# Twenty-two experts' weights copied to bfloat16 ahead of the expert stage, output weights prepared beside the projections, u2 stored by the sync queue

## What is computed

```
ada   = silu(c) @ w_ada + b_ada                  # 6 rows of 1024: shift, scale, gate, twice
u     = LN(x) * (1 + scale1) + shift1
q,k,v,g,p = split(u @ w_in)                      # 5 blocks of 512 columns
r     = retention(rotary(q), rotary(k), v)       # 4 heads of 128, chunks of 128 tokens
mix   = [silu(g) * groupnorm(r) | pool(p) @ w_pool] @ w_out
x     = LN(ALPHA * x + gate1 * mix, ln1_w, ln1_b)
u2    = LN(x) * (1 + scale2) + shift2
y     = top-1 group of 4, top-2 of its 8 gated-MLP experts (32 experts, hidden 256)
out   = LN(ALPHA * x + gate2 * y, ln2_w, ln2_b)
```

## Time and profile before

| | us |
|---|---|
| time, median of 3 runs | 1021.09 (1010.62, 1021.09, 1047.54) |
| profiled execution, its own time | 1010.89 |
| profiled execution, span of the slowest core (core 1) | 1009.1 |
| spans of the 8 cores | 981.3 to 1009.1 |
| busy: PE, DVE, ACT, POOL | 654.3, 530.5, 332.4, 351.6 |
| DMA queues, share of 16 engines over the span: q0 (POOL's), q1 (SP's) | 57.7%, 14.8% |

### The profile page before, as it was taken

The page is one execution under the profiler, slowest core; times in us unless marked ns, Lnnn a source line. Parts: engine busy times, 40 slices in busy tenths (PEclk is TensorE's granted clock), DMA queues, the critical chain, the costliest instruction groups (busy, mean ns, idle before and its releaser), DMA issues.

```text
span 1009.1 us, 11200 instructions; the slowest of 8 cores (981.3 to 1009.1 us)
## 1 busy us (share of the span) xinstructions
PE 654.3 (65%) x4072; PEld 380.4 (38%) x4072; DVE 530.5 (53%) x1222; ACT 332.4 (33%) x561; POOL 351.6 (35%) x382
## 2 busy tenths in 40 slices
PE   0259987479896798988667687667666765760000
PEld 0215554245554455446556343333323332420000
DVE  0884575257366697789876242233223322333867
ACT  3245556234433243233312232323322321321211
POOL 1214332123131122233314465354445444326112
PEclk9979898779897898887556987879978978995555
DMA  9999989843646126696311179889899699668995
GB/s 174 224 196 182 150 141 158 137 82 66 144 75 136 48 68 136 114 231 116 63 20 29 36 195 173 238 186 194 197 221 239 123 242 251 128 173 242 276 289 240
DMA packets 50934, 159.79 MB, mean 158 GB/s; under 512 B 15802, under 2 KB 16314, under 8 KB 49216
## 3 DMA queue, kind: packets, MB, share of 16 engines
q0 software_dynamic: 38496, 108.27, 57.7%
q1 hardware_dynamic: 12384, 50.80, 14.8%
HBM read 305.75 MB, written 58.20 MB: 361 GB/s over the span
## 4 chain that ended last, share of the span: by engine, by line
DMA 36%; PE 35%; DVE 12%; ACT 6%; issue 5%; POOL 5%; another core or an unknown queue 0%; POOLq 0%; DVEq 0%
DMA M<-w 10%; PE pp L1120 9%; PE pp L599 6%; DMA M<-ytok 5%; DMA M<-w_in 5%; DMA M<-w,M 4%; DMA M<-w_ada 4%; DMA M<-x 4%; PE pp L640 3%; PE pp L1137 3%; PE pp L830 3%; POOL RC L559 2%; DMA u2d<-M 2%; PE pp L877 2%; PE pp L807 2%
## 5 line engine op out<-in xcount | busy, mean ns | idle before, releaser
L1120 PE MATMUL pp<-M 128*128 128x512 bf16 (+1 forms) x504 | 143.0, 439 | 56.5 <-DMA M<-w 42.0
L1142 DVE SCALAR_TENSOR_TENSOR M<-pp,M,G 128x1024 f32<-128x1024 f32 x63 | 80.4, 1283 | 112.2 <-DMA ytok<-M 56.6
L559 POOL TENSOR_TENSOR RC<-RC 128x1 f32<-128x1 f32 x64 | 55.2, 863 | 191.8 <-DVE RC L558 153.4
L599 PE MATMUL pp<-M 128*128 128x512 bf16 x384 | 101.5, 414 | 10.4 <-ACT M L570 7.3
L1120 PEld LDWEIGHTS pp<-M 128*128 128x128 bf16 x504 | 53.4, 109 | 126.8 <-issue 47.0
L1124 DVE TENSOR_TENSOR M<-pp,M 128x256 bf16<-128x256 f32 x63 | 26.7, 424 | 135.2 <-ACT M L1123 130.6
L1087 POOL DMA_INDIRECT M<-u2d,M x63 | 65.0, 1032 | 86.3 <-PE pp L1096 65.1
L1123 ACT ACTIVATE M<-pp 128x256 f32<-128x256 f32 x63 | 24.1, 384 | 206.3 <-PE pp L1120 182.6
L1144 POOL DMA_INDIRECT ytok<-M x63 | 63.8, 1012 | 58.0 <-DVE M L1142 45.0
L1137 PE MATMUL pp<-M 128*128 128x512 bf16 (+1 forms) x252 | 70.2, 407 | 21.1 <-ACT M L1133 14.3
L1098 ACT ACTIVATE M<-pp 128x1024 bf16<-128x1024 bf16 x63 | 64.1, 1021 | 44.1 <-PE pp L1096 33.3
(11 more groups left out here) (223 smaller groups left out, 1242.7 us busy)
## 6 DMA issues: line engine op xcount, KB each, us to landing
M<-w POOLq DMA_DIRECT2D x24, 1536.0 KB
M<-x SPq DMA_DIRECT2D x32, 512.0 KB, 9.9
M<-w_ada POOLq DMA_DIRECT2D x12, 1024.0 KB
wbf<-w POOLq DMA_DIRECT2D x8, 1536.0 KB
M<-wbf SPq DMA_DIRECT2D x8, 1536.0 KB, 14.8
M<-ytok SPq DMA_DIRECT2D x16, 512.0 KB, 16.4
M<-ytok POOLq DMA_DIRECT2D x16, 512.0 KB
out<-M SPq DMA_DIRECT2D x16, 512.0 KB, 14.0
```

The source lines that it names most:

```text
L559: P.op("pool", lambda e: e.tensor_tensor(out=rs, in0=rs, in1=negh[:, 0:1], op=ALU.pow), [key + "rs", "negh"], [key + "rs"], 0.65)
L599: pe([lambda e, kc=kc: e.matmul(pb(bank), lhsT=u[:, kc, is_], rhs=wsl[blk][:, kc, :], start=(kc == 0), stop=(kc == 7)) for kc in range(8)] ...
L1120: return e.matmul(pb(bk), lhsT=uTg[pr][:, k, :], rhs=w13[:, k, :], start=(k == 0), stop=(k == 7))
L1142: dve(lambda e: e.scalar_tensor_tensor(out=yst[yb], in0=pp(yp), scalar=gslot[:, col:col + 1], in1=gate_b, op0=ALU.mult, op1=ALU.mult), ks ...
```

## The change

Four edits:

- **Copies.** `STAGED` goes from 8 experts to 22 (6 to 27). 14 copies are issued by tile in stage 2, 5 in stage 4 (behind `a5` of tiles 8, 10, 11, 13, 15, each waiting for the last operation of that `a5`, DVE L832), and 3 in the expert stage at p = 1, 2, 3. The loads of these 22 experts move from POOL to SP. The copies now carry `max_dma_last_dim=8192`.
- **ada.** `ada_chunk(4..11)` and their loads are placed one per tile at t = 1 to 8, not one every second tile to t = 15; pieces 6, 7, 10 and 11 use the slots 2 and 3, so the region of `wout` is free after piece 9.
- **Output weights.** `w_out` is loaded at t = 7, its gate row made at t = 9 and the eight pieces scaled at t = 9 to 12, not in `a5_head`.
- **u2.** ACT copies u2 to a bfloat16 buffer (`xqb`, two of them, which also take the place of `junk`), and SP stores that. Before, POOL stored the float32 tile with a cast.

```
-STAGED = [7, 10, 13, 16, 19, 22, 25, 28]
+STAGED = list(range(6, 28))
+STAGE_AT = {3: 1, 4: 1, 5: 1, 6: 1, 8: 1, 9: 1, 10: 2, 11: 1, 12: 1, 13: 1, 14: 2, 15: 1}
...
+        def ada_slot(j):
+            return j if j < 4 else (4, 5, 2, 3)[j % 4]
...
+        def scale_wout(k):
+            if k < 4:
+                dve(lambda e: e.scalar_tensor_tensor(out=wout[:, k, :], in0=wout[:, k, :], scalar=gnc[:, k:k + 1], in1=gate_b, op0=ALU.mult, op1=ALU.mult),
+                    ["gate_b", "colsb"], ["wout%d" % k], 1.2)
+            else:
+                dve(lambda e: e.tensor_tensor(out=wout[:, k, :], in0=wout[:, k, :], in1=gate_b, op=ALU.mult), ["gate_b"], ["wout%d" % k], 1.2)
...
-            P.dma("pool", lambda e: e.dma_start(out=wbf[i * 128:(i + 1) * 128, :], in_=w123[u * 128:(u + 1) * 128, :]), writes=["wb%d" % u], mb=4.2, after=after)
+            P.dma("pool", lambda e: e.dma_start(out=wbf[i * 128:(i + 1) * 128, :], in_=w123[u * 128:(u + 1) * 128, :], max_dma_last_dim=8192), writes=["wb%d" % u], mb=3.1, after=after)
...
-                if t in (3, 5, 6, 8, 9, 11, 12, 14):
+                for _ in range(STAGE_AT.get(t, 0)):
                     stage_w([len(P.ops) - 1])
...
-                if t % 2 == 1 and t < 16:
-                    j = 4 + t // 2
-                    ada_chunk(j)
-                    if j + 2 < 12:
-                        ada_load(j + 2)
+                if 1 <= t <= 8:
+                    ada_chunk(t + 3)
+                    if t + 5 < 12:
+                        ada_load(t + 5)
+                if t == 7:
+                    P.dma("pool", lambda e: e.dma_start(out=wout.rearrange("p k d -> p (k d)"), in_=w_out, max_dma_last_dim=8192), writes=["wout"], mb=4.2)
+                if t == 9:
+                    gate_row(4, gate_b, "gate_b", 1.0)
+                if 9 <= t <= 12:
+                    scale_wout(2 * t - 18)
+                    scale_wout(2 * t - 17)
...
-        junk = B("junk", S0 + 10240, 512, BF16)
+        xqb = [B("xqb%d" % i, o, 512, BF16) for i, o in enumerate((S0 + 10240, S0 + 11328))]
...
-            P.dma("pool", lambda e: e.dma_start(out=wout.rearrange("p k d -> p (k d)"), in_=w_out), writes=["wout"], mb=4.2)
-            gate_row(4, gate_b, "gate_b", 1.0)
...
-            P.dma("pool", lambda e: e.dma_start(out=u2d[t * 128:(t + 1) * 128, :], in_=xq), reads=[kx], writes=["u2d%d" % t], mb=0.5)
+            act(lambda e: e.activation(out=xqb[i], in_=xq, func=AF.Copy), [kx], ["xqb%d" % i], 1.06)
+            P.dma("sp", lambda e: e.dma_start(out=u2d[t * 128:(t + 1) * 128, :], in_=xqb[i]), reads=["xqb%d" % i], writes=["u2d%d" % t], mb=0.25)
...
+        late_copies = {8: 1, 10: 1, 11: 1, 13: 1, 15: 1}
         for t in range(8, NT):
             a5(t)
+            for _ in range(late_copies.get(t, 0)):
+                stage_w([len(P.ops) - 1])
...
         for p in range(NU + 1):
+            if staged[0] < len(STAGED) and p > 0:
+                stage_w([len(P.ops) - 1])
```

More of the change, by code:

```diff
@@ L469, in build_nc @@
         gate_b = G2[:, 0:1024]
+        def ada_slot(j):
+            return j if j < 4 else (4, 5, 2, 3)[j % 4]
         def ada_load(j):
-            sl = j if j < 4 else 4 + j % 2
+            sl = ada_slot(j)
             P.dma("pool", lambda e: e.dma_start(out=ada[sl].rearrange("p k n -> p (k n)"), in_=w_ada[:, j * 4096:(j + 1) * 4096], max_dma_last_dim=8192),
@@ L779, in a5_head @@
         def a5_head():
-            P.dma("pool", lambda e: e.dma_start(out=wout.rearrange("p k d -> p (k d)"), in_=w_out), writes=["wout"], mb=4.2)
-            gate_row(4, gate_b, "gate_b", 1.0)
-            for k in range(8):
-                if k < 4:
-                    dve(lambda e, k=k: e.scalar_tensor_tensor(out=wout[:, k, :], in0=wout[:, k, :], scalar=gnc[:, k:k + 1], in1=gate_b, op0=ALU.mult, op1=ALU.mult),
-                        ["gate_b", "colsb"], ["wout%d" % k], 1.2)
-                else:
-                    dve(lambda e, k=k: e.tensor_tensor(out=wout[:, k, :], in0=wout[:, k, :], in1=gate_b, op=ALU.mult), ["gate_b"], ["wout%d" % k], 1.2)
             P.dma("sp", lambda e: e.dma_start(out=ln1w_b, in_=ln1w.partition_broadcast(128)), writes=["ln1w"], after=lastw)
@@ L813, in a5 @@
                 ["xin2%d" % (t % 4)] + mk, [ka, k1 + "s1"], 1.32)
-            act(lambda e: e.activation(out=junk, in_=at, func=AF.Square, accum_out=stat[:, c1 + 1:c1 + 2]), [ka], ["junk", k1 + "s2"], 1.25)
+            act(lambda e: e.activation(out=xqb[i], in_=at, func=AF.Square, accum_out=stat[:, c1 + 1:c1 + 2]), [ka], ["xqb%d" % i, k1 + "s2"], 1.25)
             nm, rs = ln_tail(c1, k1, LN_EPS)
@@ L818, in a5 @@
                 ["ln1b", k1 + "rs"], [ka, k2 + "s1"], 1.32)
-            act(lambda e: e.activation(out=junk, in_=at, func=AF.Square, accum_out=stat[:, c2 + 1:c2 + 2]), [ka], ["junk", k2 + "s2"], 1.25)
+            act(lambda e: e.activation(out=xqb[i], in_=at, func=AF.Square, accum_out=stat[:, c2 + 1:c2 + 2]), [ka], ["xqb%d" % i, k2 + "s2"], 1.25)
             nm2, rs2 = ln_tail(c2, k2, LN_EPS)
```

## The result

After took 1118.28 us (median of four, 1107.39 to 1122.15), before, run beside it, 1029.45 us (1010.62 to 1047.54): a ratio of 1.099, 95% interval 1.092 to 1.105. I had forecast 947 us, and 0.86 for faster.

The account below looks back on a forecast made before the run. Transfers, not PE, were taken to set the expert stage; elsewhere DMA, PE, DVE and two holes bound. -53 - 17 - 10 + 5 + 2 = -73 gave 938 us, times 1.01 a 947 us median; range 900 to 1000.

Parts of the forecast that it names:

- Expert stage: 590 to 910 us: 14 cheaper loads at unchanged DMA share gain 59, net -53 us after copies; ends -80 and -20.
- the last sentence of the prediction: Failure signs: copies over 12 us of engines, POOL's copy waits ahead of idle DVE, or early expert loads with pace over 5 us a unit.
- A copy took 8.0 us almost alone: Price of a copy, used for six more before 304 us: with 11 us more, 59 us needed against 59 idle.
- the x hole: 182 to 208 us: x load lands sooner, -10 us, ends -18.8 and 0; a copy there priced at 10.8 us.
- the front +5: Added cost up to 304 us: +2 for gate-row matmuls, +3 for transfer backlog; ends 0 and +18.
- the page: Skill page behind the page's-price rival: 13.2 us a copy, engines full from 100 to 545, some 20 us worse; chance 0.08.
- w_out and its scaling: 304.47 to 328.95 us: load wait and 9.4 us of DVE work leave, -17 us; ends -9.4 and -24.5.
- Stage 4: u2 store -4 us and five late copies +6 us, net +2 us.
- u2 at -4: Stage 4: the u2 store's one DVE wait of 4.03 us goes, -4 us.
- The late copies, charged +6: Stage 4: five copies make POOL wait for DVE L832, 1.2 us each; ends 0 and 64 us.
- my slower rival: Stage 4 and expert stage: eight copies each hold POOL 12.8 us with DVE standing, 102 us, time 1060; chance 0.06.
- The chances: Whole kernel: under 1000 us 0.86, 1000 to 1041 0.08, over 0.06; forecast as it stands 0.54.

Follow-up runs that it names:

- a_order: After plus one order dependence on PE: a unit's first matmul stands behind the second matmul of two units earlier; 1043.44 us.
- a_lat: After with only the planner's guessed landing time of an indirect weight load made 4.0 us longer, same instructions in another order; 1066.02 us.
- the edge: The one dependence a_order adds to after: a unit's first matmul behind the second matmul of two units earlier on PE; 1043.44 us.
- b_wout_u2: After with before's eight copies, without the limit, so the ada, output-weight and u2 parts alone; 1006.91 us, 1.4% under before.
- b_u2: Before with the u2 edit alone; 1024.79 us, ratio 0.997 to 1.006.
- c11: After with eleven copies, all before the end of the pooling tiles, plus the edge; 993.68 us, 2.3% under before.

## Where the prediction was wrong

**The step that failed most** is in "Expert stage": "14 loads go from 8.5 to 4.8 us ... At the same 0.88 that is 261 us, a gain of 59", with an end of -80 by PE's busy time and one of -20 by gather and chain. The first half held: DMA share fell to 0.58, and a bfloat16 load landed in 6.8 us instead of the 14.8 of the earlier trace rows. But keeping the share at 0.88 supposes that the engines stay busy at the same rate. What came next was neither PE's 219 us nor the chain of gather and matmuls, but the round trip of the indirect loads in an order of PE that the planner had built from the cheaper loads. a_order and a_lat show it: they change the order alone and take 69 and 57 us out. None of my rivals had it, though the last sentence of the prediction has its sign ("expert loads land early and the pace stays over 5 us a unit"; the loop runs at 6.4): I asked which engine would be next and not what the planner would do with new costs. The term was +50 instead of -53; with the edge it is -19 with 22 copies and -22 with eleven, at my low end of -20.

**"A copy took 8.0 us almost alone"**, and "six more copies ... need 6 x 8.0 ... they fit only with a backlog": this is the mis-sized term of the front. A copy added 13.4 to 13.9 us of engine time beside other traffic, and my own bound from the x hole, 10.8, was low as well. At 13.9 us the same sum is 6 x 13.9 + 11 = 94 us, against the 59 idle. I charged the front +5 with ends 0 and +18 for the copies up to 304 us (and the gate row) and +6 for those of stage 4. The nineteen copies ahead of the mark cost it 597 - 521 = 76 us against none, and 68 to 74 against eight; the fourteen early ones 54 of them, the five of stage 4 the other 22. That this goes by engine time is read from the shares; no run changed a copy's engine time and nothing else. The Trainium skill (HBM Reference, Specifications) gives about 358 GB/s for a core when both of a pair stream, and the estimate of 13.2 us a copy from it agrees with the measurement: 4.72 MB in 13.9 us is 340 GB/s. That the shared memory is what sets it no run here shows. I had named the page, and gave it 0.08 and 20 us, because I counted only busy time on the whole front and not what waits for single transfers in it.

**The x hole** went as a wait: ACT's squares (L569, now L573) waited 6.1 us for x in 100 to 592 us where they had waited 25.6, 20.5 of them in the hole, and the x tile there took 11.78 us on the chain instead of 23.18. But PE now waits for adaLN pieces instead (50.1 us in the whole span, 30.5 before), and PE's work from 182 to 208 us rose only from 7.25 to 13.88 us. The queue moved its victim.

**w_out and its scaling**: -17 predicted, 12 us of front measured with the adaLN edit (b_wout_u2), inside the ends. Right in kind. Under 22 copies the output projection still starts at 281 us instead of 323 (medians of eight cores), and the front ends later all the same.

**Stage 4**: u2 at -4 was 0 (0.997 to 1.006). The rule of the Trainium skill (DMA: Bandwidth & Descriptors, Issuing engines are not separate DMA queues) would have made it 0, and the runs agree, though b_u2 changes more than the issuing engine: ACT gets the copies, and the store casts nothing. The late copies, charged +6, cost the front 22 us (597 - 575), and not by POOL's waits, as my slower rival had it. POOL stood 13.7 us in all at the five of stage 4, 9.68 of them at one, and 1.75 at the three of the expert stage, where the rival had 12.8 at each (and in that 12.8 us row of before DVE was idle beside a busy PE, 12.39 of the 12.90 us from 399.5, so it was no price of POOL's wait):

```profile
510.05 0.67 POOL L751 DMA_DIRECT2D wbf<-w  x1 [2.69 <-DVE M L911]
541.40 0.66 POOL L751 DMA_DIRECT2D wbf<-w  x1 [0.47 <-DVE M L842]
566.89 0.64 POOL L751 DMA_DIRECT2D wbf<-w  x1 [9.68 <-DVE M L911]
```

What stands beside it is engine time: in 455 to 592 us a DMA share of 0.84 (0.33 in the earlier trace rows from 455 to 545) and a 13.12 us u2 store on the chain. So the sign of the slower rival was right and its mechanism not.

**The chances** put 0.86 on one side although a backlog was already written down as certain ("they fit only with a backlog"). A change that doubles the traffic of a full resource to relieve the same resource later deserved a rival in which the backlog reaches PE.

## What to carry to other kernels

- Moving traffic to an earlier stage is worth only what that stage has idle, at the transfer's price *beside others*, and not at its price alone; here twelve copies would fit by the count; with eight and eleven the kernel came out 2% under before, with fourteen 0.5 to 1.4% over.
- Where a planner or a fixed order is tuned around one long transfer, making that transfer short changes the order too. Look for the shortest loop through the guessed latencies (slot free, load, use) and check each guess against its landing in the trace before believing a bound.
- A wait that repeats with the same period in the chain of waits is a loop; cut it in order or distance, not in bandwidth.

## What was not expected of the hardware

- An indirect load in the loop landed 6.5 to 8.1 us after its issue, and one on the chain at 628.98 us, where a copy runs too, after 26.56. c11's trace has a median of 9.4, after's 6.7. The Trainium skill (DMA: Bandwidth & Descriptors, Anatomy of one DMA) speaks of about 2 us of fixed cost, near the planner's 1.8, and the first indirect load of after agrees: 2.1 us, at a DMA share of 2.4%. Rows of 604.6 to 607.2 us, and then of 830.9 to 837.6, one turn of the loop:

```profile
q0 software_dynamic: 144, 0.00, 2.4%
M<-w,M POOLq DMA_INDIRECT x1, 2.1
...
q1 hardware_dynamic: 144, 1.57, 66.9%
q0 software_dynamic: 359, 0.33, 16.0%
M<-wbf SPq DMA_DIRECT2D x1, 1536.0 KB, 6.6
M<-w,M POOLq DMA_INDIRECT x1, 6.5
```

In the turn the whole of POOL's queue, gathers and scatters with it, writes 0.33 MB, where one expert would be 1.57: this load brings next to nothing in. A bfloat16 load issued in the same turn moves 1.57 MB, and the two land within 0.1 us of each other. So what the planner's guess leaves out looks like the time behind the transfer beside it, and 0.58 is a mean over full and empty parts of a turn. No run took that neighbour away, so the cause is argued and not shown.
- The same copies with unlimited packets made the front 15 us longer at about equal engine time (13.2 us a copy against 13.9). Which transfer pays was not separated.
- Why the expert stage stops at 332 to 337 us, while a_order kept 8.8 us a pair (277 us for all) in its middle, is open: c11's chain between 550 and 880 us holds six pieces of indirect load of 10.79 to 12.34 us and one of 23.40, so the loads' landing is again the first suspect, and an experiment with a third slot for them was not made.
